# A norm that moves behind its projections: raw x*g in, rstd multiplied into what comes out

## What is computed

```python
x = x + 0.5 * ml[8] * swiglu(modulate(rms_norm(x, norm3_g), ml[6], ml[7]), ffn2_w_in, ffn2_w_out)
x = rms_norm(x, final_g)              # end of the first block
h = rms_norm_2(x, norm_mix)           # start of the second
proj = h @ w_in_2
q_flat, kv_flat, g_attn, u_pool, g_merge = split(proj)
a = nsa_attention(q_flat, kv_flat, g_attn, ...) @ w_branch_attn
b = pool_mixer(u_pool, pool_w, pool_scale) @ w_branch_pool
ga, gb = split(sigmoid(g_merge))
x = x + (ga * a + gb * b) @ w_out
```

## Time and profile before

| | |
|---|---|
| median of 3 runs | 1299.78 us (1299.53 to 1304.49) |
| the profiled execution | 1298.4 us, its span 1296.6 us |
| TensorE, weight loads | busy 1276.1 us (98%), 1152.3 us (89%) |
| VectorE, ScalarE, GpSimd | busy 812.9 us (63%), 589.4 us (45%), 62.7 us (5%) |
| HBM | 212.24 MB read, 165 GB/s over the span |

### The profile page before, as it was taken

How to read it: one execution, slowest core, us unless ns; L and a number is a source line. 1 busy time by engine, 2 the same in 40 slices (tenths; PEclk the granted TensorE clock), 3 DMA queues, 4 the chain that set the end, 5 groups by cost and what they waited for, 6 DMA issues and landing times.

```text
span 1296.6 us, 23081 instructions
## 1 busy us (share of the span) xinstructions
PE 1276.1 (98%) x8852; PEld 1152.3 (89%) x8852; DVE 812.9 (63%) x1294; ACT 589.4 (45%) x885; POOL 62.7 (5%) x72
## 2 busy tenths in 40 slices
PE   8999999999999999999999999999999999999998
PEld 6788888888886899888999999999998889999997
DVE  3777778753345655776676555656667767566664
ACT  2543124322233336544445656546455565544542
POOL 2000000000001000000001000002013102000001
PEclk8999999999999999999999999999999999999999
DMA  9655554443225244323445454544532235455452
GB/s 380 250 195 195 195 195 193 176 193 125 88 103 195 68 151 171 131 98 100 175 179 219 149 210 168 194 163 162 195 131 98 98 104 186 162 186 190 179 173 86
DMA packets 30959, 214.19 MB, mean 165 GB/s; under 512 B 3376, under 2 KB 4656, under 8 KB 5936
## 3 DMA queue, kind: packets, MB, share of 16 engines
q1 hardware_dynamic: 30320, 211.83, 45.1%
q10 hardware_dynamic: 576, 1.48, 0.3%
HBM read 212.24 MB, written 1.05 MB: 165 GB/s over the span
## 4 chain that ended last, share of the span: by engine, by line
PE 87%; DVE 5%; ACT 3%; DMA 2%; issue 2%; POOL 0%; DVEq 0%; ACTq 0%; SPq 0%; POOLq 0%
PE ps_u L1521 26%; PE ps_u L1522 26%; PE ps_u L1523 26%; DVE w_lo L852 1%; PE ps_a L1452 1%; DMA wide_scr<-in_mods 1%; DMA raw<-in_stream 1%; ACT w_hi L487 1%; PE ps_a L1690 1%; DVE sq L929 1%; PE ps_a L1485 1%; PE ps_a L1675 1%; PE ps_a L1856 1%; PE ps_a L1463 1%; PE ps_a L1501 0%
## 5 line engine op out<-in xcount | busy, mean ns | idle before, releaser
L1521 PE MATMUL ps_u<-x_hi,w_hi 128*128 128x256 f32 (+1 forms) x1744 | 541.3, 310 | 2.8 <-DVE x_lo L940 2.2
L1522 PE MATMUL ps_u<-x_lo,w_hi 128*128 128x256 f32 (+1 forms) x1744 | 535.0, 307 | 0.0
L1523 PE MATMUL ps_u<-x_hi,w_lo 128*128 128x256 f32 (+1 forms) x1744 | 534.8, 307 | 0.0
L852 DVE TENSOR_TENSOR w_lo<-raw,w_hi 128x1024 fp32r<-128x1024 f32 x322 | 394.4, 1229 | 217.9 <-ACT w_hi L487 216.3
L487 ACT ACTIVATE w_hi<-raw 128x1024 fp32r<-128x1024 f32 x322 | 337.4, 1054 | 295.5 <-PE ps_u L1523 240.9
L1521 PEld LDWEIGHTS ps_u<-x_hi,w_hi 128*128 128x128 f32 x1744 | 333.5, 191 | 25.1 <-issue 7.7
L1522 PEld LDWEIGHTS ps_u<-x_lo,w_hi 128*128 128x128 f32 x1744 | 333.6, 191 | 15.3 <-issue 0.5
L1523 PEld LDWEIGHTS ps_u<-x_hi,w_lo 128*128 128x128 f32 x1744 | 333.6, 191 | 15.1
L1521 PE MATMUL ps_u<-h_hi,w_hi 128*128 128x256 f32 (+1 forms) x800 | 246.0, 307 | 0.9 <-DVE h_lo L1007 0.6
L1522 PE MATMUL ps_u<-h_lo,w_hi 128*128 128x256 f32 (+1 forms) x800 | 245.1, 306 | 0.0
L1523 PE MATMUL ps_u<-h_hi,w_lo 128*128 128x256 f32 (+1 forms) x800 | 245.0, 306 | 0.0
(11 more groups left out here) (241 smaller groups left out, 865.9 us busy)
## 6 DMA issues: line engine op xcount, KB each, us to landing
raw<-in_stream SPq DMA_DIRECT2D x153, 1024.0 KB, 4.8
wide_scr<-in_mods SPq DMA_DIRECT2D x18, 1024.0 KB, 7.1
scr<-in_mods SPq DMA_DIRECT2D x18, 1024.0 KB, 6.9
raw<-in_stream SPq DMA_DIRECT2D x8, 768.0 KB, 4.1
x<-in_tokens SPq DMA_DIRECT2D x2, 1024.0 KB, 6.5
wide_scr<-in_cmp_w SPq DMA_DIRECT2D x2, 1024.0 KB, 8.1
sq<-in_cmp_w SPq DMA_DIRECT2D x2, 1024.0 KB, 6.0
out<-x SPq DMA_DIRECT2D x4, 256.0 KB, 2.2
```

Of the source, the lines that this page charges most:

```text
L852: dve.tensor_tensor(w_lo[:, k % 2, cols], raw[:, k % 2, cols], w_hi[:, k % 2, cols].bitcast(F32), ALU.subtract).then_inc(l_ready, 1)
L1521: pe.matmul(dst, wh, xh, start=(kc == 0), stop=False)
L1522: pe.matmul(dst, wh, xl, start=False, stop=False)
L1523: ins = pe.matmul(dst, wl, xh, start=False, stop=(kc == span - 1))
```

## The change

It does four things.

1. In the last four output units of ffn2, ScalarE and VectorE no longer prepare squares for GpSimd: they make x_hi and x_lo of x*g (g = `gg`, both gains) for each pair of chunks at once, in `out_parts`, which `wout2` now uses too. The operands lie in the columns S to NB of x_hi and x_lo, and the projections read them there (`mix_in`).
2. `kcvc` follows ffn2 directly, without filler. The sums of squares come behind it: 16 matmuls with two moving columns (1 and g squared, `sq_gain`), which replace GpSimd's adding and the second set of squares. The spread stands behind the gate logits.
3. rstd is multiplied in later: into the rope tables, into the two banks of `kcvc`, the logits, v, and the pool input (which were copies), by VectorE, from a copy `r_mix`.
4. The merge gates leave PSUM by a VectorE product with `r_mix` instead of ScalarE's copy and VectorE's tick. The second set of compression weights waits for the sums of squares instead of x_lo.

```diff
             run(FIRST["kcvc"], FIRST["kcvc"] + 4)
-            sp.wait_ge(xl_ready, 4 * KD)
+            sp.wait_ge(stat_done, 4)
             cmp_weights(1)
...
             sums(2, S)
-            sums(3, NB)
...
+            def out_parts(k, m, gain):
+
+                split(0, k + 2, 0)
+                act.wait_ge(drained, k + 3)
+                for t in range(2):
+                    act.activation(x_hi[:, m + t, S:NB], x[:, m + t, 0:S], ACT.Identity, scale=gain(m + t)).then_inc(xh_ready, 1)
+                split(0, k + 2, 1)
+                for t in range(2):
+                    act.activation(sq[:, m + t, 0:S], x[:, m + t, 0:S], ACT.Square).then_inc(sq_ready, 1)
...
                     for i in range(4):
-                        out_step(pr, k + chunks, i, n, gain if last else None, last)
+                        if last and mixed_next:
+                            if i == 1:
+                                prepare_root()
+                            out_parts(k + chunks + i, 2 * i, lambda m: gg[:, m:m + 1])
+                        else:
+                            out_step(pr, k + chunks, i, n, last)
...
-            swiglu(FIRST["ffn2"], 22, S, V_F1)
-            splits(0, FIRST["kcvc"] + 1)
+            swiglu(FIRST["ffn2"], 22, S, True)
+            splits(0, FIRST["kcvc"] + 2)
             act.wait_ge(var_steps, 3)
             act.activation(root[:, 0:4], var[:], ACT.Sqrt).then_inc(root_done, 1)
-            norm_hi(3, S, None)
...
-            splits(0, k + 2)
-            act.wait_ge(gt_done, 1)
+            act.wait_ge(gt_scaled, 1)
             act.activation(g_feat, ps_a[0:3 * H2, 1, 0:S], ACT.Sigmoid).then_inc(gt_sig, 1)
...
                 split(r, kg + 2, 0)
-                gates_out(r, g)
...
+            def lo_parts(n, m, gain):
+                for t in range(2):
+                    dve.wait_ge(xh_ready, 8 * n + m + t + 1)
+                    dve.scalar_tensor_tensor(x_lo[:, m + t, S:NB], x[:, m + t, 0:S], gain(m + t),
+                                             x_hi[:, m + t, S:NB].bitcast(F32), ALU.mult, ALU.subtract).then_inc(xl_ready, 1)
+
+            def out_parts(n, k, m, gate, gain):
+
+                split(0, k + 2, 0)
+                add_out(0, k, m, S, gate)
+                if m:
+                    lo_parts(n, m - 2, gain)
+                if m == KD - 2:
+                    lo_parts(n, m, gain)
+                split(0, k + 2, 1)
...
-            split(0, FIRST["kcvc"] + 1, 0)
+            splits(0, FIRST["kcvc"] + 2)
+            for t in range(2):
+                dve.memset(cmp_in[t][:, :, :, NC:NCP], 0.0)
             dve.wait_ge(stat_done, 4)
...
             spread(3, 4)
-            split(0, FIRST["kcvc"] + 1, 1)
-            norm_lo(3, 3, S, lambda kc, s: gg[:, kc:kc + 1], None, S)
+            dve.wait_ge(rb_done, 4)
+            r_wide = ps_a[:, 2, S:NB]
+            dve.tensor_copy(r_mix, r_wide).then_inc(rmix_ready, 1)
+            dve.tensor_tensor(cos2_r, cos2, r_wide, ALU.mult)
+            dve.tensor_tensor(sin2_r, sin2, r_wide, ALU.mult).then_inc(tables_scaled, 1)
+            dve.wait_ge(rmix_ready, 1)
...
             for t in range(2):
-                dve.memset(cmp_in[t][:, :, :, NC:NCP], 0.0)
+                dve.tensor_tensor(bank(k, t), bank(k, t), r_mix, ALU.mult).then_inc(kv_scaled, 1)
+            for t in range(2):
+                dve.wait_ge(kv_scaled, t + 1)
...
-            split(0, k + 2, 1)
+            dve.wait_ge(gt_done, 1)
+            logits = ps_a[0:3 * H2, 1, 0:S]
+            dve.tensor_tensor(logits, logits, r_mix[0:3 * H2, :], ALU.mult).then_inc(gt_scaled, 1)
...
                 split(r, kg + 2, 0)
-                dve.wait_ge(g2_copied, h + 1)
-                dve.tensor_copy(tick[:], eps).then_inc(drained, 1)
+                done(r, kg)
+                dve.tensor_tensor(gates2[:, 2 * r + g, :, :], ps_u[:, 2 * (kg % 2):2 * (kg % 2) + 2, 0:S],
+                                  r_mix.unsqueeze(1).broadcast_to([P, 2, S]), ALU.mult).then_inc(drained, 1)
...
             swiglu(FIRST["ffn2"], 2, S)
-            keep_busy(6)
-            stat(3, 4)
-            keep_busy(4)
-            spread(3, 4)
-            keep_busy(5)
...
             k = FIRST["kcvc"]
-            unit(0, k, from_x(S), ready=normed(3))
+            unit(0, k, mix_in, ready=normed(3))
+            for kc in range(KD):
+                pe.wait_ge(sq_ready, KD * 3 + kc + 1)
+                for t in range(TT):
+                    ins = pe.matmul(ps_a[:, 3, t:t + TT + 1:TT], sq[:, kc, t * P:(t + 1) * P], sq_gain[:, kc, :],
+                                    start=(kc == 0 and t == 0), stop=(kc == KD - 1 and t == TT - 1))
+            ins.then_inc(stat_done, 1)
...
             ins.then_inc(gt_done, 1)
+            spread(3, 4)
```

More of the change, by code:

```diff
@@ L414, in sums @@
             def sums(n, width):
+                made = n if n < 3 else n - 1
                 for kc in range(1, SUMMED):
@@ L523, in norm_hi, with squares, out_step @@
                     for s, cols in segs(n):
-                        if shift is None:
-                            ins = act.activation(x_hi[:, kc, cols], sq[:, kc, cols], ACT.Copy)
-                        else:
-                            ins = act.activation(x_hi[:, kc, cols], sq[:, kc, cols], ACT.Identity,
-                                                 bias=mods[:, shift * KD + kc, s:s + 1])
+                        ins = act.activation(x_hi[:, kc, cols], sq[:, kc, cols], ACT.Identity,
+                                             bias=mods[:, shift * KD + kc, s:s + 1])
                     ins.then_inc(xh_ready, 1)
-            def squares(pr, k, m, n, gain=None):
+            def squares(pr, k, m, n):
                 act.wait_ge(drained, 2 * pr + (k + 3))
                 for t in range(2):
-                    if gain is not None:
-                        act.activation(sq[:, m + t, S:NB], x[:, m + t, 0:S], ACT.Square, scale=vcol(gain, m + t))
                     act.activation(sq[:, m + t, 0:n], x[:, m + t, 0:n], ACT.Square).then_inc(sq_ready, 1)
-            def out_step(pr, k0, i, n, gain=None, last=True, more=True):
+            def out_parts(k, m, gain):
[6 more added lines that the diff above has]
+                    act.activation(sq[:, m + t, 0:S], x[:, m + t, 0:S], ACT.Square).then_inc(sq_ready, 1)
+            def out_step(pr, k0, i, n, last=True, more=True):
                 if last and i == 1:
@@ L798, in _ @@
             for i in range(4):
-                k, m = FIRST["wout2"] + i, 2 * i
                 if i == 1:
                     prepare_root()
-                split(0, k + 2, 0)
-                act.wait_ge(drained, k + 3)
-                for t in range(2):
-                    act.activation(x_hi[:, m + t, S:NB], x[:, m + t, 0:S], ACT.Identity, scale=vcol(V_MLP, m + t)).then_inc(xh_ready, 1)
-                split(0, k + 2, 1)
-                for t in range(2):
-                    act.activation(sq[:, m + t, 0:S], x[:, m + t, 0:S], ACT.Square).then_inc(sq_ready, 1)
+                out_parts(FIRST["wout2"] + i, 2 * i, lambda m: vcol(V_MLP, m))
             roots(4, 2)
@@ L822, in relu2 @@
                 for i in range(4):
-                    out_step(pr, k + 4, i, S, None, last, not (last and i >= 2))
+                    out_step(pr, k + 4, i, S, last, not (last and i >= 2))
             with act.Fori(0, SLABS2 - 1) as s:
@@ L1013, in pairs, with outs @@
                             pair(pr + p, k + j, c + 2 * p + j, 2 * p + j, j)
-                def outs(pr, k, last):
+                def outs(pr, k):
                     for o in range(4):
-                        out_step(pr, k, o, n, gate, last)
+                        out_step(pr, k, o, n, gate, False)
                 if n == NB:
@@ L1408, in _ @@
             for i in range(4):
-                k, m = FIRST["wout2"] + i, 2 * i
-                split(0, k + 2, 0)
-                add_out(0, k, m, S, None)
-                for t in range(2):
-                    dve.wait_ge(xh_ready, 8 * 4 + m + t + 1)
-                    dve.scalar_tensor_tensor(x_lo[:, m + t, S:NB], x[:, m + t, 0:S], vcol(V_MLP, m + t),
-                                             x_hi[:, m + t, S:NB].bitcast(F32), ALU.mult, ALU.subtract).then_inc(xl_ready, 1)
-                split(0, k + 2, 1)
+                out_parts(4, FIRST["wout2"] + i, 2 * i, None, lambda m: vcol(V_MLP, m))
             spread(4, 2)
@@ L1454, in stat @@
             def stat(n, tiles):
+                made = n if n < 3 else n - 1
                 for kc in (*range(SUMMED, KD), 0):
                     if kc == 0:
-                        pe.wait_ge(sq_sums, (SUMMED - 1) * (n + 1))
+                        pe.wait_ge(sq_sums, (SUMMED - 1) * (made + 1))
                     else:
@@ L1744, in _ @@
             for kc in range(KD):
-                pe.matmul(dst, wg_hi[:, kc, :], x_hi[:, kc, 0:S], start=(kc == 0), stop=False)
```

(14 more changed lines are left out.)

77 lines of the change are left out of this document (41 added, 36 removed).

## The result

The changed kernel takes 1303.32 us (median of 20 executions, 1301.33 to 1306.86), the kernel before 1299.65 us, measured beside it (20 executions, 1295.07 to 1304.49). The ratio is 1.0032 with a 95% interval of 1.0021 to 1.0043: slower by 4.2 us, within the 0.5% that I had set as a bound, but 0.8 us above the range of 1296.0 to 1302.5. The profiled execution took 1305.0 us, its span is 1303.2 against 1296.6. That pair is 6.6 us apart, and 1.2 us of it stand ahead of ffn2 already, where the change does nothing (the first filler ahead of ffn2 starts at 699.9 instead of 698.7).

What follows compares the result with a forecast made beforehand. TensorE was taken to bound the kernel, busy 1276.1 of 1296.6 us. The norm's -3.1, the merge gates' +1.1 and the clock's +1.7 sum to -0.3 us, hence 1299.5 against a median of 1299.78; range 1296.0 to 1302.5.

Steps and rivals of the forecast that it cites:

- The ring: ScalarE and VectorE cycle of weight splits, adds, x_hi and squares in ffn2's last units: 5.56 us against units of 4.32.
- O3 late: Last output unit of ffn2's last slab starts 0.3 us late, waiting for a bank that an add frees.
- The hole: TensorE wait of 3.4 us within unit `kcvc`, at its fifth chunk, until x_lo is made.
- The open sums: Sums of squares behind `kcvc`, now uncovered: 32 passes taking 3.68 us.
- what covers the spread: Diagonal ready at 914.5, before the gate logits end at 915.1; if not, up to 1 us more.
- The spread's own price: Spread matmul behind the gate logits: 0.43 us at full clock, from 0.86 in the slow stretch.
- The clock at the norm: One clock fall behind the sums, over gate logits and `ksvs`: +1.7 us, bounds 0 and 3.4.
- The merge gates: VectorE's gate product delays head 1's transposes: +1.1 us, nothing passed on in later heads; bounds 0 and 4.4.
- the clock falls twice: Rival, 15%: the wait in `kcvc` and the sums behind it each cost 1.7 us of clock: 1301.2 us.
- the engines keep up: Rival, 10%: ScalarE and VectorE don't hold TensorE around `kcvc`: 1292.8 us, or 1294.5 with the clock.
- every head is pushed: Rival, 6%: the gate product delays every head because VectorE sets the head's period: +6.3 us, 1306.1.
- K1's weights: Rival, 8%: weights of `ksvs` land late, at 6.2 us, lengthening the wait in `kcvc` by 1.3: some 1302.8 us.

Runs made afterwards that it cites:

- e6: Changed kernel with VectorE's merge-gate product moved into the next head, where VectorE waits for exponentials; 1301.48 us, ratio 1.0010 to the kernel before.
- e2: Changed kernel with low pieces and the last pair's pieces made ahead of the second projection unit's weight splits; 1300.72 us, ratio 1.0005 to the kernel before.
- e3: Changed kernel with 28 filler matmuls put ahead of chunk 4 of `kcvc`; 1311.87 us, ratio 1.0090 to the kernel before.
- e5: Changed kernel with the sums of chunks 0 to 3 moved ahead of chunk 4 of `kcvc`; 1299.67 us, ratio 1.0001 to the kernel before.
- e9: Changed kernel with sum passes alternating with gate-logit matmuls and the spread inside `ksvs`; 1301.82 us, ratio 1.0017 to the kernel before.
- e7: Changed kernel with merge gates copied by ScalarE again and not scaled by rstd; 1300.99 us, ratio 1.0010 to the kernel before.
- e8: Changed kernel with the edits of e2 and e6, and sums of chunks 0 to 5 spread within `kcvc`; 1297.51 us, ratio 0.9984 to the kernel before.
- e13: e8 run once more, unaltered, for a second trace; 1300.10 us in one execution.
- e10: e8 plus the spread inside `ksvs` and rotary tables scaled behind the compressed inputs; 1294.93 us, ratio 0.9961 to the kernel before.

## Why the prediction was wrong

By its own steps, with the times relative to where each begins:

- **The ring: right.** Split a every 5.58 and 5.74 us where 5.56 was worked out from the earlier trace rows; O3 late (0.35 us of wait at 895.33), K0 held by the adds.
- **The hole: right.** K0 started at 900.90, 899.42 was worked out and 1.2 us of the difference stand ahead of ffn2; 0.3 us are left that I had not. The hole ends 6.24 us behind K0's start (907.14), where 6.3 was worked out (905.7 less 899.42), and x_lo releases it.
- **The open sums and what covers the spread: right. The spread's own price: wrong.** At full clock 32 passes take 3.67 us (e6), 3.68 was worked out. The diagonal was ready in time. But I read the spread's 0.86 us as its time at the low clock and halved it, and the clock was back at 1.00 when it ran:

```profile
907.92 2.32 PE L1474 MATMUL ps_a<-cst,ones 128*128 128x256 f32 x10
907.00:911.00 4.00, 4.00 (x21) 3.23 (x21) 2.79 (x8) 1.56 (x4) 0.00 (x0) 1.00 0.70 258
```

  These are the row behind the spread and the window around it, in the kernel before. At full clock the spread costs 0.86, so 0.4 us more than my term. In the new trace this shows one matmul behind K1's start (921.30, the next at 921.82).
- **The clock at the norm: the step that failed.** I counted one fall, at +1.7. There are two. The first is of that size, 1.4 of it over useful work; the second is twice as long. K0's second half took 4.27 us instead of 2.88 (+1.4), the sums 4.72 instead of 3.68 (+1.0), the logits 4.71 instead of 2.77 (+1.9): 4.4 us, 2.7 more than my term, and more than its upper bound of 3.4. From K0's start to K1's my sum gives 17.8 us with the term (915.5 less 899.42, and 1.7) and the trace has 20.4. The difference of 2.6 is the clock alone. e2, e3, e5 and e9 take the two falls apart: the first goes when the hole goes, the second when the thin passes no longer stand 32 in a row. I had taken the size of a fall from the only one in the earlier trace rows and had no row for one that lasts longer, and I had put the hole's fall among the rivals.
- **The merge gates: right in kind, short in size.** The product pushed head 2's transposes by 1.58 us (2.74 less 1.16), not 1.1. Two products of 0.60 for ticks of 0.06 make 1.1; VectorE's second split in head 0 takes 1.54 instead of 1.35, and 0.54 us instead of 0.15 pass between reciprocal and gate product in head 1. Why these two are longer wasn't tried. As forecast, the later heads pass nothing on.
- **The clock in the heads: not in the prediction.** The longer wait comes just ahead of eight transposes, the clock falls, and the transposes (1.60 instead of 0.82 us) and the unit's first matmuls cost 1.4 us more (0.8 and 0.6). e6 and e7 show that the longer wait goes with the product's place, and in their traces the fall goes too. But the fall doesn't hang on the product alone: e5 and e9 with the product in its place, and e8 and e13 with it moved, have a fall at head 1's transposes instead of head 2's, and an H of 82.6 to 82.7 us in all four.

In the pair of traces the terms that I had not or had too small sum to 2.6 (clock at the norm) + 0.4 (spread) + 0.3 (K0's start) + 0.5 (gates) + 1.4 (clock in the heads) = 5.2 us, on a forecast of -0.3: 4.9 slower, where P and H give 4.8. The ratio over all executions gives 4.2. The rival "the clock falls twice" named the right mechanism, with 1.7 for each fall and nothing in the heads; its 1301.2 us is 2.1 below the result. The Trainium skill, TensorE: Matmul & The Clock Gate, What's actually happening, which stood beside it, speaks of activity that releases the throttle and of an idle engine that goes back to 1.2 GHz. The hole agrees with this (3.1 us idle, then 0.61). The sums of e3 go beyond it, since TensorE issued without a pause there. That VectorE's second place in the ring holds the time was right; "the engines keep up" is out, "every head is pushed" too (10.57 us in later heads), and K1's weights were not late.

Still open: why e5, e8, e9 and e13 show a fall in head 1, where the 1.72 us from scores to transposes are the same as in the kernels that show none, and why the second fall at the norm is shorter in e6 and e7.

## What to carry to other kernels

When filler matmuls go, price the clock over the useful work that now stands in their place, at both levels: each fall of the changed kernel cost 1.4 to 2.9 us of it, and at the norm the falls followed the hole and the unbroken thin stretch. Put thin matmuls (sums over one or two columns) one chunk at a time among wide ones; in e8, e9 and e10 they then cost their passes and nothing behind them. An operation that moves to another engine belongs where that engine waits: in the traces the same eight products went with 2.9 us in the chain and with nothing 5 us later in the gap. And when one value comes late, look at all its readers in order: e10 put the tables behind the compressed inputs and then waited for the gate logits, which stood behind the tables.
